# Sums, a weight remainder and late parameters in another order in the first layer of a two-block kernel

## The reference, cut to what matters

```
def ada_mod(c, w, b):
    return jnp.einsum('bd,de->be', jax.nn.silu(c), w) + b

for layer in range(DEPTH):
    sh1, sc1, g1, sh2, sc2, g2 = jnp.split(ada_mod(c, ada_w[layer], ada_b[layer]), 6, axis=-1)
    h = modulate(rmsnorm(x, norm_mix_g[layer]), sh1, sc1)
    y = mlstm_mixer(h, ...)                       # layer 0; layer 1: stick-breaking attention
    x = x + g1[:, None, :] * y
    h = modulate(rmsnorm(x, norm_ffn_g[layer]), sh2, sc2)
    x = x + g2[:, None, :] * peer_ffn(h, ...)

# in mlstm_mixer
proj = jnp.einsum('bsd,de->bse', h, w_in)         # qk, v, o, gates
qk = jax.nn.silu(causal_conv(qk, conv_w))
w_state = b_last[..., None] - b + i_pre           # gates: log_sigmoid, cumsum, running max
hh = num / jnp.maximum(jnp.abs(den), jnp.exp(-m_t))[..., None]
hh = rmsnorm(hh, hnorm_g) * jax.nn.sigmoid(o)
```

## Time and profile before

| what | value |
|---|---|
| median of three runs | 2536.04 us (2535.36 to 2536.52) |
| the profiled execution, its own time | 2536.82 us |
| its span in the trace | 2535.0 us |
| TensorE busy | 2494.9 us, 98% of the span |
| VectorE busy | 2040.5 us, 80% |
| ScalarE busy | 1492.4 us, 59% |
| GpSimd busy | 345.5 us, 14% |
| chain that ended last | TensorE 87%, VectorE 5%, DMA 4%, ScalarE 2%, issue 1%, GpSimd 1% |

### The profile page before, as it was taken

How to read it: one execution, slowest core, us unless ns; L and a number is a source line. 1 busy time by engine, 2 the same in 40 slices (tenths; PEclk the granted TensorE clock), 3 DMA queues, 4 the chain that set the end, 5 groups by cost and what they waited for, 6 DMA issues and landing times.

```text
span 2535.0 us, 44017 instructions
## 1 busy us (share of the span) xinstructions
PE 2494.9 (98%) x14932; PEld 2170.5 (86%) x14932; DVE 2040.5 (80%) x3770; ACT 1492.4 (59%) x2489; POOL 345.5 (14%) x212
## 2 busy tenths in 40 slices
PE   7999999999999999999999999999999999999998
PEld 6789988888888888889988888888888888899887
DVE  7789979899888877679888998666667886688766
ACT  4455576666666656555677666665564555463553
POOL 4017600000000003527500000000000001000000
PEclk8999999999999999999999999999999999999999
DMA  7854576776888885435666776566555355553654
GB/s 270 284 167 165 195 238 191 201 208 204 302 292 288 284 258 162 142 122 170 210 217 193 206 199 209 183 200 202 194 191 190 127 188 184 193 177 107 199 183 141
DMA packets 142991, 509.07 MB, mean 201 GB/s; under 512 B 19200, under 2 KB 19256, under 8 KB 142560
## 3 DMA queue, kind: packets, MB, share of 16 engines
q1 hardware_dynamic: 135600, 481.90, 57.3%
q0 software_dynamic: 7216, 24.85, 5.1%
HBM read 488.84 MB, written 1.07 MB: 193 GB/s over the span
## 4 chain that ended last, share of the span: by engine, by line
PE 87%; DVE 5%; DMA 4%; ACT 2%; issue 1%; POOL 1%; SPq 0%; DVEq 0%; ACTq 0%
PE ps L243 51%; PE ps L249 19%; PE ps L250 9%; DMA weight_ring<-in_stream 4%; PE ps L1528 2%; ACT weight_split L269 1%; DVE weight_split L278 1%; POOL weight_split L278 1%; PE ps L2735 1%; PE ps L1492 1%; DVE arena L745 0%; DVE hT_split L503 0%; PE ps L457 0%; DVE stat L628 0%; DVE x L625 0%
## 5 line engine op out<-in xcount | busy, mean ns | idle before, releaser
L269 ACT ACTIVATE weight_split<-weight_ring 128x1024 fp32r<-128x1024 f32 x800 | 848.8, 1062 | 224.5 <-DMA weight_ring<-in_stream 132.9
L243 PE MATMUL ps<-weight_split,hidden_split 128*128 128x512 f32 x3948 | 911.8, 390 | 0.4 <-DVE hidden_split L1821 0.3
L278 DVE TENSOR_TENSOR weight_split<-weight_ring,weight_split 128x1024 fp32r<-128x1024 f32 x653 | 791.4, 1221 | 135.2 <-ACT weight_split L269 132.0
L243 PEld LDWEIGHTS ps<-weight_split,hidden_split 128*128 128x128 f32 x3948 | 736.0, 188 | 157.1 <-issue 1.0
L249 PE MATMUL ps<-hT_split,weight_split 128*128 128x512 f32 x2000 | 721.9, 402 | 0.5 <-DVE hT_split L503 0.4
L250 PE MATMUL ps<-hT_split,weight_split 128*128 128x256 f32 x2000 | 559.5, 280 | 0.0
L243 PE MATMUL ps<-hT_split,weight_split 128*128 128x256 f32 x3672 | 462.8, 285 | 3.0 <-DVE hT_split L503 0.8
L243 PEld LDWEIGHTS ps<-hT_split,weight_split 128*128 128x128 f32 x3672 | 447.3, 192 | 10.3 <-issue 5.9
L249 PEld LDWEIGHTS ps<-hT_split,weight_split 128*128 128x128 f32 x2000 | 375.7, 188 | 84.5 <-DVE hT_split L503 1.1
L250 PEld LDWEIGHTS ps<-hT_split,weight_split 128*128 128x128 f32 x2000 | 377.8, 189 | 2.6
L278 POOL TENSOR_TENSOR weight_split<-weight_ring,weight_split 128x1024 fp32r<-128x1024 f32 x115 | 279.1, 2433 | 115.5 <-ACT weight_split L269 85.2
(11 more groups left out here) (381 smaller groups left out, 2078.3 us busy)
## 6 DMA issues: line engine op xcount, KB each, us to landing
weight_ring<-in_stream SPq DMA_DIRECT2D x912, 512.0 KB, 4.2
weight_split<-weight_ring POOLq DMA_DIRECT2D x32, 512.0 KB, 5.3
arena<-gate_rows SPq DMA_DIRECT2D x3, 512.0 KB, 4.8
x<-in_x SPq DMA_DIRECT2D x1, 1024.0 KB, 5.1
arena<-mlstm_m_rows POOLq DMA_DIRECT2D x1, 1024.0 KB, 6.5
arena<-in_ln_mix_g POOLq DMA_DIRECT2D x2, 512.0 KB, 5.8
arena<-in_ln_mix_b POOLq DMA_DIRECT2D x2, 512.0 KB, 7.8
arena<-in_ln_ffn_g POOLq DMA_DIRECT2D x2, 512.0 KB, 4.7
```

Source lines behind the costliest of these rows:

```text
L243: mm = pe.matmul(out_, stationary(s_part), moving(m_part), start=start and n == 0, stop=stop and n == 2, skip_group_check=True)
L269: act.activation(wsplit[:, n % SPLITS, HIGH, :], ring[:, slot(POS[n]), :], ACT.Copy).then_inc(high_ready, 1)
L278: eng.tensor_tensor(w[:, REST, :], ring[:, slot(POS[n]), :], w[:, HIGH, :].bitcast(fp32), ALU.subtract).then_inc(split_ready, 1)
```

## The change

Five things are written in another order. Nothing is computed that was not computed before.

1. The four late parameters (mask 128 KB, sel and pick 32 KB each, hnorm 4 KB) are no longer loaded with the first three but when 12 sums are done; their readers wait for all seven, the readers of the first three for three.
2. GpSimd does rest 4 ahead of moving the running maximum out, and not behind it.
3. Sum 16 stands behind the convolution of column tile 5, sum 17 behind the whole convolution and ahead of rest 10.
4. Sum 18 stood ahead of rest 11, and the sums 19 to 23 each behind one of the rests 11 to 15. Now the sums 18 to 22 stand behind the rests 11 to 15, and sum 23 behind sum 22.
5. In the residual with rms 2, the reciprocal root and the scaling of the first half of row tile 0 stand behind the last additions.

```diff
@@ residual_dve
             gated(1, low)
             added(1, low).then_inc(x_third, 1)
             if rms is not None:
-                rms_rstd_dve(rms, 0)
-                rms_tok_dve(0, low)
+                if rms != 2:
+                    rms_rstd_dve(rms, 0)
+                    rms_tok_dve(0, low)
             dve.wait_ge(tiles_used, done_tiles)
             gated(1, high_)
             added(1, slice(512, 768)).then_inc(x_third, 1)
             added(1, slice(768, D)).then_inc(x_ready, 1)
             if rms is not None:
+                if rms == 2:
+                    rms_rstd_dve(rms, 0)
+                    rms_tok_dve(0, low)
                 rms_bias_dve(rms)
@@ mlstm_pool
-            for dst, src in ((ml_wg, io["ml_wg"]), (ml_bif, io["ml_bif"]), (ml_conv_w, io["ml_conv_w"]), (ml_mask, io["ml_mask"]),
-                             (ml_sel, io["ml_sel"]), (ml_pick, io["ml_pick"]), (ml_hnorm, io["ml_hnorm"])):
+            for dst, src in ((ml_wg, io["ml_wg"]), (ml_bif, io["ml_bif"]), (ml_conv_w, io["ml_conv_w"])):
                 pool.dma_start(dst, src).then_inc(ml_par, 16)
-            rests_pool(ML_T + 1, 3)
+            pool.wait_ge(ml_par, 16 * 3)
+            pool.wait_ge(ada_used, 12)
+            for dst, src in ((ml_hnorm, io["ml_hnorm"]), (ml_mask, io["ml_mask"]), (ml_sel, io["ml_sel"]), (ml_pick, io["ml_pick"])):
+                pool.dma_start(dst, src).then_inc(ml_par, 16)
+            rests_pool(ML_T + 1, 4)
 
             pool.wait_ge(ml_gate_dve, M_READY)
             pool.dma_start(ml_rows.rearrange("(h t) -> h t", t=T), ml_M).then_inc(ml_M_moved, 16)
-            for n in range(ML_T + 4, ML_T + 6):
-                rest(pool, n)
+            rest(pool, ML_T + 5)
             pool.wait_ge(ml_M_moved, M_OUT)
@@ mlstm_pe, mlstm_act, mlstm_dve: the first readers
-            pe.wait_ge(ml_par, 16 * 7)
+            pe.wait_ge(ml_par, 16 * 3)
...
-            act.wait_ge(ml_par, 16 * 7)
+            act.wait_ge(ml_par, 16 * 3)
...
-                    dve.wait_ge(ml_par, 16 * 7)
+                    dve.wait_ge(ml_par, 16 * 3)
@@ mlstm_dve
+            dve.wait_ge(ml_par, 16 * 7)
             after_dve(dve.tensor_scalar(ml_hnorm, ml_hnorm, 0.5, None, ALU.mult))
...
                 last.then_inc(ml_conv, 1)
-            ada_dve(16, ml_acc[:, 1])
+                if c == 5:
+                    ada_dve(16, ml_acc[:, 1])
+            ada_dve(17, ml_acc[:, 1])
             splits_until(dve, ML_T + 10)
             rest(dve, ML_T + 10)
-            ada_dve(17, ml_acc[:, 1])
...
-            ada_dve(18, ml_acc[:, 1])
             for c in range(3, 8):
                 rest(dve, ML_T + 8 + c)
-                ada_dve(16 + c, ml_acc[:, 1])
+                ada_dve(15 + c, ml_acc[:, 1])
+            ada_dve(23, ml_acc[:, 1])
             weigh(0)
```

More of the change, by code:

```diff
@@ L1090, in mlstm_pe @@
             pe.wait_ge(ml_cols_ready, 1)
+            pe.wait_ge(ml_par, 16 * 7)
             def values(h):
```

## The result

The changed kernel takes 2540.75 us, the median of 15 runs (2538.46 to 2542.16). The kernel before took 2536.2 us in 15 runs (2535.28 to 2538.91). The ratio is 1.0017, with an interval of 1.0010 to 1.0024. So the change loses a little: 0.17%, and by the interval between 0.10 and 0.24%. The prediction was 2539.8 us, in a range of 2534.0 to 2542.2.

A forecast was written before the change was run, and what follows sets the result against it. The first layer was taken as bound by how soon ring slots come free, with TensorE full from 104 us. Terms +0.1 + 3.9 - 0.25 = +3.75 gave 2540.6 us profiled, 2539.8 as median; range 2534.0 to 2542.2.

The forecast's parts named there:

- the hold: Gates: VectorE's addition L1298, both inputs in SBUF, waits for GpSimd's rest 4 and ends 2.1 us later.
- third case: Gates: addition L1298 starts first and does not wait for rest 4; 2.1 us less, 2537.7 us; chance 0.15.
- the issue: Convolution: s tile 12's load goes out 2.1 us sooner by earlier sums, cancelled by the late addition, so at 72.8.
- A round: First layer, from one s tile's load to the next of its chain: 1.8 us longer by a sum and an issue.
- step to head 1: End of the first layer: later loads and sums bring TensorE's first product of head 1 to 107.8, +3.9 us.
- second case: First layer: a 27's load takes 7.09 us again as loads pile up; +5.8 there, 2541.7 us; chance 0.17.
- the +0.1: Start: value taken for loading the late parameters later, sum 4 gaining up to 0.29 us, sum 15 losing up to 0.57.
- The case of short loads: First layer: loads of 3.2 us keep rounds from growing; 2533.6 us, or 2535.8 with the hold; chance 0.17.
- The sum: Whole kernel: +0.1 + 3.9 - 0.25 = +3.75 us on the profiled execution's 2536.82, so 2540.6; median 2539.8.

The follow-up runs named there:

- e1: Kernel before with only GpSimd's rest 4 put ahead of moving the running maximum out; 2541.1 us, ratio 1.0012.
- e6: Changed kernel with the addition of the gates' sum to their running maximum moved behind the convolution's fourth column tile; 2538.72 us, 1.0008 to the kernel before.
- e9: Changed kernel timed and profiled once more, with no edit; 2540.91 us, ratio 1.0019 to the kernel before.
- e10: Changed kernel with only the sums 18 to 23 put back to their old places; 2536.85 us, ratio 1.0002 to the kernel before.
- e3: Kernel before with only the sums 16 and 17 moved up; 2535.25 us, ratio 0.9993.
- e2: Kernel before with only the sums 16 to 23 ordered as in the changed kernel; 2540.45 us, ratio 1.0014.
- e5: Kernel before with only the sums 18 to 23 moved, each behind a later rest; 2540.59 us, ratio 1.0017.
- e7: Kernel before with only the four late parameters loaded when 12 sums are done; 2536.2 us, ratio 0.9999.
- e4: Kernel before with only the scaling behind the first experts moved; 2537.46 us, ratio 1.0001.

## Why the prediction was right, and where it was not

**Part 2, the hold: right in mechanism and size.** +2.1 was said. The addition grew by 2.03 us (0.41 to 2.44) and ended 0.3 us behind rest 4, at 52.41 (said: 52.1, and the whole row of operations started 0.4 late). e1 shows the hold with part 2 alone, and e6 takes it away by giving VectorE a step that reads PSUM. The third case, "not held", has fallen: in after, e1, e9 and e10, the four executions with rest 4 ahead and the addition in its place, it took 2.44 us each time. The Trainium skill, "SBUF — State Buffer", "SBUF: two separate sides", lets the one who starts first go through. The trace agrees only if rest 4 counts as first: it is queued behind rest 3 while VectorE is still in its scan.

What the step left out is TensorE. In those four executions it was busy 0.65, 0.92, 0.54 and 0.38 us of the window from 56 to 59, where before it was 3.00 of 3: it did column tile 4 early and then waited for tile 5. In three of the four the granted clock went to 0.50 behind it, in the first not. That nothing is won by TensorE's early start on tile 4 was right. But the pause has a price. At the lower clock the 24 matmuls behind it came onto the chain (4.64 us in e9, 4.66 in e10, 4.65 in e1), and the convolution's next steps waited for them, 3.6 us in place of 2.1. From the start of rest 5 to the issue of s 12 lie 16.86 us in after, and 18.39 in e9 and 18.09 in e10, which have the same code up to there: 1.5 and 1.2 us more. So part 2 costs 2.0 us by the hold, and up to 1.5 us more in an execution in which the clock falls. The profile of after happens to be one in which it did not.

**Part 3: right for the issue, wrong in the length of sum 16.** s 12 went out at 72.81 us (said: 72.8). To hit it that closely was luck, since e9 and e10, with the same code up to there, have 75.42 and 74.30. Without part 2 the part gives 1.4 to 1.9 us there (e3, e2; said: 2.1). But sum 16 took 3.53 us and not 1.22. Its two inputs lie in SBUF, and it met rest 8, the last of three in a row that end at 65.97 us on GpSimd, and ended 1.1 us behind it, as the addition had met rest 4. I had applied the hold to L1298 and not to the sum that part 3 moves beside a rest. It cost nothing here, as in after VectorE made up for it: six steps of the convolution ran back to back behind it, at 67.00.

**Part 4: right, and without it there is no loss.** A round was to grow by 1.8 us, the sum 1.22 and an issue 0.6. From the issue of s 12 to that of s 14 lie 9.04 us (before 6.87), to that of s 16 another 9.23 (before 7.48): 2.2 and 1.75 more. s 14 went out at 81.85 (said: 81.4), s 16 at 91.08 (said: near 90.5), and in e5 at 81.29 and 90.50. Undone in e10, it takes 4.1 us off the time, and what is left, part 2 against part 3, comes to 1.0002. The step to head 1 was too large by 1.1 us: +2.84 at head 1 in place of +3.9. The odd tiles had come as said (s 13 at 78.19 for 78.1, s 15 at 86.60 for 86.7), but the load of s 15 took 3.95 us where I had put 4.4, and rest 15 ended at 92.8 and not 93.5; a 24 landed after 4.12 us in place of 4.6. Sum 24 thus ended 1.2 us sooner than said. The last load took 5.38 us where I took 5.1, so the second case, 7.09 again, did not come. The reason given for it is not shown: at the issue of that load three others were in flight before and in after alike. In the executions with the old order of the sums 18 to 23 it took 5.04 to 7.09 us, with the new one 5.37 to 6.17, so the 7.09 that the prediction started from lay at the upper end of what this load takes.

**Part 1: too small at both ends.** Sum 4 won 0.50 us and not at most 0.29: its wait went, and sum 3 had found its tile 0.13 us sooner too (12.23 us in place of 12.36), which I had left out. This gain is there in all six executions with part 1 (sum 4 at 14.27 to 14.36 us; at 14.50 to 14.82 in the eight without). It is not kept: sum 15 starts at 31.97 to 32.46 us in the eight without part 1, and at 30.91 to 33.48 in the six with it. So -1.1 to +1.5 was seen where -0.3 to +0.6 was said, with the middle near the +0.1. What part 1 seems to do is to spread that start, not to shift it; six executions don't prove it, and no effect on the median was found (e7).

**Part 5: right in mechanism, a little more in size.** -0.36 us in place of -0.25, from the distance of TensorE's matmuls around the turn, in e4 as in after.

**The case of short loads.** It has fallen: behind 60 us the ring's loads took 4.4 us in the median in after, and 3.2 only at best. The section "Anatomy of one DMA" of the Trainium skill, "DMA: Bandwidth & Descriptors", from which the 3.2 us came, gives its sum for transfers that GpSimd issues. The ring's loads are issued by SyncE, so it was no figure for them.

**The sum.** +3.15 us in the profiled executions (said: +3.75). Of that 2.84 came at head 1 and -0.36 in the turn. The remaining 0.7 is no effect of the change: 1.06 arose between 316 and 377 us, in the first experts, where the code is the same. Between the same two matmuls lie 58.15 us in before and again in e9, which is the changed kernel, and 59.20 in after and in the other executions. So +3.75 and +3.15 lie close in part by luck: the +3.9 at head 1 was 1.1 too large, and 1.06 of chance came on top. The matmuls in a window of 58 us show the two paces, here before:

```profile
316.00:374.00 58.00, 58.00 (x339) 51.24 (x338) 45.22 (x54) 44.95 (x64) 0.00 (x0) 1.00 0.75 254
```

and here e4, with 332, where after has 333 in the window three microseconds later:

```profile
316.00:374.00 58.00, 58.00 (x332) 50.39 (x331) 44.92 (x54) 44.39 (x62) 0.00 (x0) 1.00 0.76 251
```

Smaller differences of both signs (+0.5 near 694 us, -0.5 near 942, -0.3 near 1660) make up the rest.

**What stays open.** The medians differ by 4.55 us and the profiles by 3.15, and for the kernels with part 4 or the held addition the medians lost 1.3 to 2 us more than head 1 did (e1 +1.5 and +3.5, e2 +1.5 and +2.8, e5 +2.4 and +4.2). Most of this is the profile before, whose last load took 7.09 us: at the issue of a 27 the losses are 4.55 in after and 2.86, 2.40 and 4.06 in e1, e2 and e5. That the first equals the median's to the hundredth is chance. The medians of the parts alone also add up, -0.2 (part 1), +3.5, -2.4, +4.2 and -0.15 to +4.95 against +4.55, while head 1 gives +1.0 against +2.84. Each median is uncertain by about 2 us, so no more can be asked. The low clock takes a share that was not measured by itself: 1.2 to 1.5 us by the issue of s 12 in e9 and e10, and e1 and e5 had a fall at 79.5 and 75.8 us as well. Why the clock falls in one execution and not in another, and why the load of a 27 took 5.04 to 7.09 us, was not settled.

## What to carry to other kernels

Where a ring of slots is refilled in strict order, the instruction that releases the slot ahead belongs before the work whose load is awaited and not behind it: one reduction of 1.2 us put behind each remainder lengthened every round by about 2 us. Before an operation with both inputs in SBUF is put into VectorE's idle time, look at what GpSimd does in that time; one that reads PSUM can stand there, and moving a 0.4 us addition behind such steps brought the ring's loads 2.0 us forward (s 12 in e6). One part can be a gain and another the loss: without part 4 the change costs nothing (1.0002), and part 3 alone lies 2.4 us below before, though its interval still holds 1. So time each part alone before judging the whole, and don't count gains of one or two us from a single profile of the kernel before.

## What the runs showed of the hardware

- VectorE operations with both inputs in SBUF that met a rest of GpSimd were stretched and ended behind it: an addition from 0.41 to 2.44 us, a scan from 0.68 to 2.79, a sum of 128x1024 from 1.22 to 3.53, and later in before an addition of 128x385 (L2154) from 0.56 to 2.59. The steps with PSUM as an input kept 0.48 to 0.49 us beside rest 4, in e6 as in before. Not everything that reads SBUF is held: the index searches (FIND_INDEX8) of L1701, with one SBUF tensor of 128x128, took 0.28 to 0.29 us in before, beside rests and away from them.
- The granted clock fell to 0.50 for about 3 us in some executions and not in others of the same kernel (after without, e9 with it at 59.6 us), each time behind a stretch in which TensorE had been idle for about half the time or more: busy 0.69 us of 3.6 in e9, 0.94 of 3.0 in e5, 2.36 of 4.5 ahead of the second fall in e1. Before was busy 0.72 of 2.8 us from 73 us on, and its clock stayed.
- The same loop of matmuls ran at one of two paces, 58.15 or 59.20 us for the same stretch, at a granted clock of 1.00 in both, and one kernel showed both (after, e9). This moves a single profile by 1 us and is as large as most parts of this change.
